# A state-space loop in eight steps of two pairs, interleaved with the retention projection, and its scalar chain computed one stage earlier

## The reference

```
lam_bar = exp(lam * dt);  b_bar = (lam_bar - 1) / lam * B
x[t] = lam_bar * x[t-1] + b_bar u[t]          # both directions, context first, then latent
y    = D u + sum over directions of Re(C x)
out  = gelu(y) * sigmoid(gelu(y) @ glu_w + glu_b)
```

## Time and profile before

| | us |
|---|---|
| median of 3 runs | 2098.81 |
| the profiled execution | 2097.79 |
| its span | 2096.0 |
| TensorE busy in the span | 1909.9 (91%) |
| VectorE busy in the span | 1262.9 (60%) |
| ScalarE busy in the span | 676.7 (32%) |
| GpSimd busy in the span | 150.9 (7%) |

### The profile page before, as it was taken

The page is one execution under the profiler, slowest core; times in us unless marked ns, Lnnn a source line. Parts: engine busy times, 40 slices in busy tenths (PEclk is TensorE's granted clock), DMA queues, the critical chain, the costliest instruction groups (busy, mean ns, idle before and its releaser), DMA issues.

```text
span 2096.0 us, 26354 instructions
## 1 busy us (share of the span) xinstructions
PE 1909.9 (91%) x9912; PEld 1582.9 (76%) x9912; DVE 1262.9 (60%) x2050; ACT 676.7 (32%) x868; POOL 150.9 (7%) x179
## 2 busy tenths in 40 slices
PE   5999999988656567999999999999999999999998
PEld 2788888867545445788888877888888797679998
DVE  4777677368799735477667637775433434545554
ACT  2522122251222144332222234221222433444443
POOL 0000000100254400200000010000001000010001
PEclk8999999999777789899999999999999999999999
DMA  6453453322000020255445334534323341023453
GB/s 273 181 194 142 165 220 138 105 86 75 21 1 0 1 90 23 78 192 185 155 176 212 112 110 161 200 138 163 120 78 122 112 151 41 1 81 141 167 192 121
DMA packets 39809, 257.99 MB, mean 123 GB/s; under 512 B 4800, under 2 KB 5952, under 8 KB 14784
## 3 DMA queue, kind: packets, MB, share of 16 engines
q1 hardware_dynamic: 39744, 257.13, 33.7%
HBM read 256.06 MB, written 1.05 MB: 123 GB/s over the span
## 4 chain that ended last, share of the span: by engine, by line
PE 83%; DVE 10%; ACT 3%; issue 3%; DMA 1%; DVEq 0%; POOL 0%; SPq 0%; ACTq 0%; POOLq 0%
PE ps_all L1524 24%; PE ps_all L1528 24%; PE ps_all L1525 24%; PE bank L1667 2%; DVE w_lo L858 2%; PE ps_all L1813 2%; PE bank L1824 2%; DVE cprod L433 1%; PE bank L1572 1%; ACT w_hi L537 1%; DMA start_scale<-in_w_scale 1%; PE bank L1803 1%; PE ps_all L1803 1%; PE bank L1852 1%; PE bank L1743 1%
## 5 line engine op out<-in xcount | busy, mean ns | idle before, releaser
L1524 PE MATMUL ps_all<-a_hi,w_lo 128*128 128x512 f32 (+1 forms) x1808 | 666.4, 369 | 46.2 <-DVE w_lo L858 20.5
L1525 PE MATMUL ps_all<-a_hi,w_hi 128*128 128x512 f32 (+1 forms) x1808 | 661.8, 366 | 0.0
L1528 PE MATMUL ps_all<-a_lo,w_hi 128*128 128x512 f32 (+1 forms) x1808 | 661.4, 366 | 0.2 <-DVE a_lo L989 0.2
L858 DVE TENSOR_TENSOR w_lo<-w_raw,w_hi 128x2048 fp32r<-128x2048 f32 (+3 forms) x184 | 376.6, 2047 | 189.7 <-ACT w_hi L537 183.1
L1524 PEld LDWEIGHTS ps_all<-a_hi,w_lo 128*128 128x128 f32 x1808 | 347.6, 192 | 108.2 <-DVE w_lo L858 26.0
L537 ACT ACTIVATE w_hi<-w_raw 128x2048 fp32r<-128x2048 f32 (+3 forms) x183 | 313.4, 1713 | 357.0 <-PE ps_all L1528 348.6
L1528 PEld LDWEIGHTS ps_all<-a_lo,w_hi 128*128 128x128 f32 x1808 | 347.5, 192 | 57.4 <-DVE a_lo L989 4.1
L1525 PEld LDWEIGHTS ps_all<-a_hi,w_hi 128*128 128x128 f32 x1808 | 348.0, 192 | 52.3
L870 DVE SCALAR_TENSOR_TENSOR mod_junk<-mod_raw,cond 128x1024 bf16<-128x1024 f32 x256 | 302.8, 1221 | 1.8 <-DMA mod_raw<-in_w_mod 1.1
L1528 PE MATMUL ps_all<-g_lo,w_hi 128*128 128x512 f32 (+1 forms) x704 | 260.4, 370 | 0.0
L1524 PE MATMUL ps_all<-g_hi,w_lo 128*128 128x512 f32 (+1 forms) x704 | 256.9, 365 | 0.7 <-DVE w_lo L858 0.7
(11 more groups left out here) (199 smaller groups left out, 1688.6 us busy)
## 6 DMA issues: line engine op xcount, KB each, us to landing
w_raw<-in_tiles SPq DMA_DIRECT2D x118, 1024.0 KB, 4.8
mod_raw<-in_w_mod SPq DMA_DIRECT2D x64, 1024.0 KB, 4.8
w_raw<-in_tiles SPq DMA_DIRECT2D x32, 768.0 KB, 4.0
w_raw<-in_tiles SPq DMA_DIRECT2D x32, 640.0 KB, 3.7
start_raw<-in_w_mod SPq DMA_DIRECT2D x4, 1024.0 KB, 16.0
start_scale<-in_w_scale SPq DMA_DIRECT2D x4, 1024.0 KB, 20.2
bias<-in_na_bias SPq DMA_DIRECT2D x2, 1536.0 KB, 8.6
h<-in_h SPq DMA_DIRECT2D x1, 2048.0 KB, 16.2
```

The costliest lines, as they stand in the source:

```text
L858: nc.vector.tensor_tensor(w_lo[:, slot, 0:size], w_raw[:, slot, 0:size], w_hi[:, slot, 0:size].bitcast(F32), ALU.subtract).then_inc(lo_rea ...
L1524: pe.matmul(dst, w[1], x[0], start=start, stop=False)
L1525: pe.matmul(dst, w[0], x[0], start=False, stop=False)
L1528: return pe.matmul(dst, w[0], x[1], start=False, stop=stop_)
```

## The change

- The scalar chain (`prepare`) moves into the eight tiles of `ffn0.down1`, the last segment ahead of the mixer: tile t takes the t-th part of it, on VectorE between `split_lo` of the next tile and the residual. Its small loads move with it, and `pt` lies in `stat`.
- Tables are no longer made for all pairs. ScalarE makes the angles, sines and cosines of two pairs per step (`angles`, `sines`; 128x512), VectorE one operation between (`fraction`).
- `build_w` and `build_c` work on two pairs at a time, with instructions twice as wide and half as many.
- The kernel products of a pair are 7 matmuls in place of 16. ScalarE lays the four shifted rows (`kernel_rows`, four copies for a pair); VectorE's `kernel_tile` is gone. The skip term comes in by a matmul.
- Outputs go to `bank[0]`, states to `bank[1]` and `bank[2]`. So `ps` is free, and each of the first seven steps holds one tile of `ret_in` (tile 0 lies ahead of the loop), cut in two parts. Rope is inside the loop, in steps 0 to 3, in place in PSUM.
- Gelu is taken pair by pair. The buffer `y` is now in `cond`, which is loaded and passed through silu again in `ffn1.up0`.
- The lag table is still loaded when the last output is made. Loops on these engines are written out.

The core of the diff (the body of `prepare`, not shown, has the operations of the removed chain in the same order; the powers are copied in 8 instructions where there were 36):

```diff
             def mixer0():                       # TensorE
-                for j in range(6):              # ret_in tiles 0 to 5, swaps for rope between
-                    ...
-                turn_w(0, 0)
-                inputs_to_state(0, 0)
-                for q in range(4):
-                    pair_body(0, q)
-                ...
-                outputs(15, 1, 3, 3)
-                pe.wait_ge(S["gelu"], 4)
-                for j in (6, 7):
-                    pair_tile("ret_in", j, 8, 0)
+                for part in range(2):
+                    input_tile(0, part)
+                pe.wait_ge(S["pads"], 1)
+                turn_w(0)
+                turn_w(1)
+                inputs_to_state(0)
+                inputs_to_state(1)
+                pe.wait_ge(S["skip"], 16)
+                kernel_products(0)
+                kernel_products(1)
+                for b in range(8):
+                    if b < 4:
+                        swaps(b)
+                    if b < 7:
+                        input_tile(b + 1, 0)
+                        turn_w(2 * b + 2)
+                    outputs(2 * b)
+                    if b < 7:
+                        turn_w(2 * b + 3)
+                        inputs_to_state(2 * b + 2)
+                        input_tile(b + 1, 1)
+                        inputs_to_state(2 * b + 3)
+                    outputs(2 * b + 1)
+                    if b < 7:
+                        kernel_products(2 * b + 2)
+                        kernel_products(2 * b + 3)
             def mixer0():                       # VectorE
-                build_w(0, 0)
-                build_c(0, 0)
-                pair_body(0, 0, True)
-                ...
-                dve.wait_ge(S["y"], 16)
-                split_lo(base + 6, 2048, 0)
-                split_lo(base + 7, 2048, 1)
-                split_lo(base + 8, width("glu"), 0)
+                build_w(0)
+                fraction(0)
+                build_c(0)
+                split_lo(base + 1, 2048, 1)
+                for b in range(8):
+                    rotate(2 * b)
+                    turn_back_sine(2 * b)
+                    if b < 7:
+                        build_w(b + 1)
+                    split_lo(base + b + 2, 2048 if b < 6 else width("glu"), b % 2)
+                    rotate(2 * b + 1)
+                    turn_back_sine(2 * b + 1)
+                    if b < 7:
+                        fraction(b + 1)
+                        build_c(b + 1)
+                    if b < 4:
+                        rope(b)
             def mixer0():                       # ScalarE
+                for b in range(8):
+                    kernel_rows(2 * b)
+                    kernel_rows(2 * b + 1)
+                    if b:
+                        gelu(2 * b - 1)
+                    split_hi(base + b + 2, 2048 if b < 6 else width("glu"), b % 2)
+                    if b < 7:
+                        angles(b + 1)
+                        turned(2 * b + 2)
+                        turned(2 * b + 3)
+                    gelu(2 * b)
+                    if b < 7:
+                        sines(b + 1)
+                    if b < 5:
+                        evacuate(b + 1)
+                    ...
+                gelu(15)
+                evacuate(7)
             def mixer0():                       # GpSimd
+                build_c(0)
+                for b in range(8):
+                    turn_back(2 * b)
+                    if b < 7:
+                        build_c(b + 1)
+                    turn_back(2 * b + 1)
             ...                                 # VectorE, down("ffn0.down1")
                         mod_beside(segment, it, slot, between)
+                        if segment == "ffn0.down1":
+                            prepare(2 * it + slot)
                         residual(n, slot, 2 * it + slot, 1, FFN_T0[f])
```

More of the change, by code:

```diff
@@ L600, in step @@
                                 square(k_norm, 2 * t - 2 + m, m)
-                if "down" in segment:
+                if segment == "ffn0.down1":
+                    for t in range(tiles):
+                        step(t, t % 2, t == 0)
+                        prepare(t)
+                elif "down" in segment:
                     step(0, 0, True)
@@ new lines, in gelu @@
+                def gelu(pair):
+                    m, q = pair // 4, pair % 4
+                    act.wait_ge(S["y"], pair + 1)
+                    for t in range(4):
+                        ins = nc.scalar.activation(y[32 * q:32 * q + 32, m, t::4],
+                                                   bank[0][32 * t:32 * t + 32, q * P:(q + 1) * P], ACT.Gelu_apprx_tanh)
+                    ins.then_inc(S["gelu"], 1)
+                angles(0)
+                split_hi(base + 1, 2048, 1)
+                sines(0)
@@ L1194, in rotate, with build_c @@
-                def rotate(pair, slot):
+                def build_c(b):
+                    dve.wait_ge(S["w"], b + 1)
+                    to = [prod[:, 320 * n:320 * n + 320] for n in range(2)]
+                    c_products(nc.vector, b, to, ((0, 0), (1, 1))).then_inc(S["cprod"], 1)
+                    dve.wait_ge(S["cprod"], b + 1)
+                    if b >= 2:
+                        dve.wait_ge(S["y"], 2 * b - 2)
+                    c_combine(nc.vector, b, 0, to, add).then_inc(S["c"], 1)
@@ L1195, in rotate, with fraction @@
+                def fraction(b):
+                    dve.wait_ge(S["magic"], b + 1)
+                    nc.vector.scalar_tensor_tensor(tsin[:, b % 2], tcos[:, b % 2], MAGIC, tsin[:, b % 2], sub,
+                                                   sub).then_inc(S["frac"], 1)
+                def rotate(pair):
+                    c, slot = 2 * pair, pair % 2
                     v = bank[1 + slot][:].rearrange("p (d r j) -> p d r j", d=2, r=2)
+                    r = [r4[:, c + d:c + d + 1] for d in range(2)]
@@ L1238, in pair_body @@
-                def pair_body(pair, slot, more):
-                    if more:
-                        build_w(pair + 1, 1 - slot)
-                    kernel_tile(pair, slot)
-                    rotate(pair, slot)
-                    turn_back_sine(pair)
-                    if more:
-                        build_c(pair + 1, 1 - slot)
-                build_w(0, 0)
-                build_c(0, 0)
-                pair_body(0, 0, True)
-                pair_body(1, 1, True)
-                with dve.Fori(1, 7) as it:
-                    for slot in range(2):
-                        pair_body(2 * it + slot, slot, True)
```

716 lines of the change are left out of this document (352 added, 364 removed).

## The result

The changed kernel takes 1997.61 us, the median of four runs (1995.47 to 1997.80), beside 2099.76 for the kernel before on the same chip (2098.44 to 2104.66). The ratio is 0.9507, 95% interval 0.949 to 0.9524. I had said 1990, range 1972 to 2017. The profiled execution took 1997.80 us, where I had said 1988.8 for such an execution; it has a span of 1996.0 us where before had 2096.0.

The account below looks back on a forecast made before the run. It took VectorE to bound the loop; first rotation at 470.2, seven steps of 162 us, last step, output, lag table and decay put first scores at 665.5, 109 us less: 1990 us, range 1972 to 2017.

Parts of the forecast that it names:

- The scalar chain in `ffn0.down1` is free: In the tiles of `ffn0.down1`, the moved chain hides in VectorE's waits for TensorE: cost nothing, ends 0 and +1 us.
- VectorE per step, with rope 24.0 and without 22.0: In the loop, a two-pair step takes 24.0 us with rope, including 5.1 for meeting GpSimd, and 22.0 without rope.
- Rival 1: In the loop, GpSimd holds VectorE up for all its time, 8.4 us a step for 5.1: 2014 us, chance 0.12.
- What bounds the steps without rope: In loop steps 4 to 6, TensorE binds with 20.4 us of its own and some 1.6 for short gaps: 22.
- TensorE's tally of 21.4: In a loop step, TensorE's tile, swaps, transposes, drives, outputs and kernel products sum to 21.4 us, 20.4 without swaps.
- "no cost" given to ScalarE's sines: In the loop, sines are ready while `build_c` and rope run: no cost; without that cover up to 3 us a step.
- The last step, 11.4: The loop's last step: two rotations, a half-wide low part and 1.5 us of meeting take 11.4 us, to 643.6.
- Last output 5.0 later: At the loop's end, the last output comes 5.0 us after VectorE's last turn back, at 648.6.
- Lag table: After the last output, its load of 7.3 us, formerly covered by tiles 6 and 7, becomes a wait, to 656.1.
- Rival 2: In the loop, TensorE's clock dips in every step, making steps of 25.4 to 26 us: 2008 us, chance 0.18.
- Rival 3: In the loop, less meeting than before: VectorE 18 to 20 us, TensorE's 20.4 to 21.4 binds: 1975 us, chance 0.14.
- Rival 4: In the loop, waits chain the engines so little overlaps, 45 us a step: 2137 us, slower than before, chance 0.04.

Follow-up runs that it names:

- e4: The changed kernel with the scalar chain back in the mixer, in one piece ahead of the first builds: 2031.25 us, 33.6 more.
- e3: The changed kernel without GpSimd's loop tensor operations and without three quarters of projection tiles 1 to 7: 1952.65 us, 45.0 less.
- e9: The changed kernel with ScalarE making the high part ahead of the kernel rows and gelu in the last step only: 1996.19 us.
- e6: The changed kernel with the lag table laid over the loop's bases, its load waiting for the last kernel product: 1994.47 us.
- e2: The changed kernel with only the first and last block of eight multiplied in projection tiles 1 to 7: 1995.08 us, 2.5 less.
- e5: The changed kernel with rope moved right behind VectorE's part of the even pair's turn back: 1996.47 us.
- e1: The changed kernel with GpSimd's tensor operations in the loop left out, one-element memsets in their place: 1957.59 us, 40.0 less.
- e10: The kernel of e8 again, timed (the changed kernel with all GpSimd loop work on VectorE): 1986.68 us, ratio to before 0.9464.
- e11: e8, e9 and e6 combined, plus the decay's logarithm in `ffn0.down1` and gates 6 and 7 copied out behind the first exponentials: 1974.35 us, ratio to before 0.9408.
- e8: The changed kernel with all of GpSimd's loop work given to VectorE, nothing left out: 1993.92 us.

## Why the prediction was right, and where it was off

The mechanism held: the loop is bound by VectorE, slowed by GpSimd, with the projection under it. The time was 7.6 us above the forecast, on the slow side in both terms that were off, and the width of the range took that in. Of the terms up to the first scores (675.09 against 665.5, 9.6 late) each can be named:

1. **The scalar chain in `ffn0.down1` is free: right.** The residuals at the end now wait less and start no later. VectorE in the changed kernel:

```profile
413.32 0.88 DVE L992 SCALAR_TENSOR_TENSOR h<-ps_all,gate,h 128x256 f32<-128x256 f32 x2 [0.70 <-PE ps_all L1558]
...
420.25 0.87 DVE L992 SCALAR_TENSOR_TENSOR h<-ps_all,gate,h 128x256 f32<-128x256 f32 x2 [0.74 <-PE ps_all L1558]
```

The last one was at 420.35 with 2.69 of idle time. Only 0.7 us of cover is left. e4 shows the worth of the move, 27.1 us at the first rotation, mainly 23.1 of chain and 4.1 of pads.

2. **First rotation at 470.2:** 469.8.

3. **VectorE per step, with rope 24.0 and without 22.0:** 25.3, and 23.3 twice and 22.2. This is the term that was mis-sized, 5.2 + 2.8 = 8.0 us in sum. Its own part was right (18.95 forecast, 19.03 in e3). The price of meeting GpSimd was taken as 5.1, scaled from what the first pair lost in the kernel before; it is 6.3, and e3 shows it in six groups of rows. That pair was the wrong one to read. In the later pairs of the kernel before, GpSimd's sums of line 440 also met VectorE's scans:

```profile
578.35 0.70 DVE L1210 TENSOR_TENSOR_SCAN sq_acc<-r,scaled 128x64 f32<-128x64 f32 x2 [0.15 <-DVE scaled L1204]
578.98 0.99 DVE L1214 TENSOR_TENSOR_SCAN sq_acc<-r,scaled 128x128 f32<-128x128 f32 x2
```

The first pair has 0.47 and 0.71 there. From rotate to the first product it was 581.10 - 576.12 = 4.98 us in this pair and 4.82 in the next, where the earlier trace rows gave 4.34. With the 2.6 of the builds a pair lost 3.1 to 3.2, 6.1 to 6.4 a step. That this comes to the 6.3 of the new loop, where other operations meet, may be chance.

   Rival 1, all of GpSimd's time, was priced at 8.4: too much. GpSimd is busy 12.07 us in the step, and every VectorE instruction beside it (from the products at 499.44 to the low part, and from the fraction to the last sums) has two inputs in SBUF. But a part of GpSimd's 12.07 is its own waiting for VectorE: its product at 498.88 ends at 500.68, 1.15 us behind the end of VectorE's turn back (498.84 + 0.69), the same distance as in the earlier trace rows, so that some 0.65 of its 1.80 is a wait. This accounts for 1.3 us a step with both products; how the rest divides isn't shown. The rule behind the rival stands in the Trainium skill (SBUF — State Buffer, "Who interferes with whom"): the port pair that the two engines share is an exclusive lock. The fraction at 513.27 agrees: it ended 0.55 us behind GpSimd's product, where it takes 0.69 alone. What failed is the step from the rule to the sum of the waits.

4. **What bounds the steps without rope:** I said TensorE. It was VectorE still: busy 22.60 of 23.4 us, TensorE 19.17, with a small wait for ScalarE's cosine at each even rotation. In the changed kernel:

```profile
594.23 0.69 DVE L1248 TENSOR_TENSOR scaled<-bank,tcos 128x512 f32<-128x512 f32 x1 [0.41 <-ACT tcos L729]
```

TensorE's tally of 21.4 took its small matmuls from rows of a stretch with the clock at 0.75. At full clock the kernel products of a pair run from 518.29 to 519.47, 1.2 us and not 1.4, and a drive is 515.91 to 516.80, 0.9 and not 1.15. The "no cost" given to ScalarE's sines was thus 0.4 us short in each step without rope, and those waits are also in term 3. With GpSimd quiet they grow to 1.50 (e3). One reading was wrong without effect: the 6.2 us that bound the last pair's outputs run from the start of the operation at 725.80, not from its end.

5. **The last step, 11.4:** 14.1, from 639.79 to VectorE's last turn back at 653.9. The missing 2.7 is a wait that the forecast didn't look for: ScalarE has the kernel rows, a table load and gelu(13) to do ahead of the high part that VectorE's low part needs, and VectorE stands 4.17 us. e9 takes it away and gains 3.0.

6. **Last output 5.0 later:** 5.1. **Lag table:** 7.0 to the first use against 7.5 (the sum has 0.2 more than the 7.3 of the earlier trace rows). My picture of it was half wrong, and that the sum came out is luck. I priced it as a bare wait; 4.9 us of it are ScalarE's own work, which would be there anyway, and moving the load alone gains 2.1 (e6). **From there to the scores:** 9.1 against 9.4.

7. **The rivals.** Rival 2 (the clock dips in every step and sets the pace) is refuted: the clock is 0.97 over the loop. It does fall in some steps, to 0.93 in the one from 495.10, with the matmul behind the waits shown below at 0.75 us long (512.80), but VectorE is the bound there. e2 adds that with the clock at 0.79 and less work the steps stay. Rival 3 (less meeting) is refuted by the steps of 25.3. Rival 4 (waits chain the engines): TensorE has two waits in order on VectorE a step, here in the changed kernel, and they are paid out of its slack:

```profile
506.19 0.66 PE L1550 MATMUL bank<-const,wb 128*128 128x128 f32 x4 [1.49 <-DVE wb L1221]
...
510.36 1.09 PE L1550 MATMUL bank<-const,wb 128*128 128x128 f32 x4 [2.39 <-DVE scaled L1249]
```

What stays open: why TensorE's clock where the second layer's attention begins is 0.79 in one execution and 0.91 in another of the same kernel. It is worth some 6 us of each total, more than most single edits here.

## What to carry to other kernels

Sum up a loop engine by engine, and give each engine its own time and its time beside the others as two terms: the first was had to 0.1 us from rows before, the second is where the forecast failed, so bound it by placing the partner's instructions under this engine's, one by one, and read the loss from a step in the middle of the loop, not from the first. Before the work of an engine is moved under another, look at what it covered: rope had hidden the wait for the cosine (e5). A second engine that holds up the bounding one is only help while it costs less than it takes over: here GpSimd's 12 us a step cost VectorE 6.3 us, and VectorE does the same work itself in 4.9. When stretches far from the edit wander by 5 to 10 us between executions, read an experiment between two events around the edit rather than by its total.

## What the runs showed that I had not expected

- GpSimd was a loss in this loop: 40.0 us in all with its work left out (e1), 10.9 us with its work given to the engine that was already the bound (e10).
- Three quarters of the seven tiles in the loop could be left out of TensorE's work (8 us a step) at no gain, while the clock fell from 0.93 to 0.79 (e2).
- ScalarE's table load is 1.28 us in every row of these traces. Three of the four between the last gelu and the exponentials moved elsewhere in e11, by the order of the gates' copies and by working the decay out earlier.
- A single total can mislead: e8 and e10 are one kernel, at 1993.92 and 1986.68 us, and from first rotation to first scores they agree within 0.5 us.
